# Four modulation units in one accumulator, 32 partitions each, against one unit at a time

## What is computed

```
cond = silu(c)                                             # 1 x 1024
mod = (cond @ w_ada[l] + b_ada[l]).reshape(b, 9, d)        # w_ada[l]: 1024 x 9216
kv_mod = (cond @ w_kv_ada + b_kv_ada).reshape(b, 2, d)     # once, for the shared K and V
h = modulate(x, mod[:, 0], mod[:, 1])                      # x * (1 + scale) + shift
x = post_norm_residual(x, swiglu(h, w_in, w_out), mod[:, 2], 0.5, ...)   # gate
```

## Time and profile before

| | us |
|---|---|
| median of 3 runs (1035.7 to 1037.51) | 1035.95 |
| span of the profiled execution | 1034.2 |
| PE busy | 1008.3 (97%) |
| DVE busy | 781.2 (76%) |
| ACT busy | 524.7 (51%) |
| POOL busy | 86.0 (8%) |
| DMA moved | 265.62 MB, 257 GB/s on average |

### The profile page before, as it was taken

How to read it: one execution, slowest core, us unless ns; L and a number is a source line. 1 busy time by engine, 2 the same in 40 slices (tenths; PEclk the granted TensorE clock), 3 DMA queues, 4 the chain that set the end, 5 groups by cost and what they waited for, 6 DMA issues and landing times.

```text
span 1034.2 us, 12480 instructions
## 1 busy us (share of the span) xinstructions
PE 1008.3 (97%) x4768; PEld 832.3 (80%) x4768; DVE 781.2 (76%) x915; ACT 524.7 (51%) x843; POOL 86.0 (8%) x160
## 2 busy tenths in 40 slices
PE   4999999999999999999999999999999999999997
PEld 3878888888888888888878888888888878888885
DVE  6888677879876897768887587777888977545485
ACT  1645453566465753545465644443568764434432
POOL 0011111000000011111000011111010010000000
PEclk9999999999999999999999999999999999999999
DMA  9999899846775499998928499989846748556541
GB/s 352 376 380 379 300 301 312 304 162 225 261 246 163 145 383 342 295 310 304 337 82 304 142 359 300 306 301 308 304 157 217 241 140 298 185 182 202 176 151 41
DMA packets 147491, 265.62 MB, mean 257 GB/s; under 512 B 8424, under 2 KB 98920, under 8 KB 147432
## 3 DMA queue, kind: packets, MB, share of 16 engines
q1 hardware_dynamic: 124448, 182.87, 52.2%
q0 software_dynamic: 20928, 75.53, 20.9%
q10 hardware_dynamic: 2056, 6.42, 1.9%
HBM read 263.75 MB, written 1.05 MB: 256 GB/s over the span
## 4 chain that ended last, share of the span: by engine, by line
PE 82%; DVE 9%; ACT 4%; issue 2%; DMA 2%; SPq 0%; DVEq 0%; ACTq 0%
PE psum L1419 17%; PE psum L1421 17%; PE psum L1420 17%; PE psum L1515 8%; PE psum L1517 8%; PE psum L1516 8%; DVE w_lo L951 2%; DMA raw<-in_w_ffn_in 2%; PE psum L1554 2%; ACT w_hi L584 1%; ACT psum L698 1%; DVE qT L1143 1%; PE psum L1454 1%; DVE qT L1144 1%; DVE tmp L972 1%
## 5 line engine op out<-in xcount | busy, mean ns | idle before, releaser
L951 DVE TENSOR_TENSOR w_lo<-raw,w_hi 128x2048 fp32r<-128x2048 f32 x164 | 371.5, 2286 | 61.2 <-ACT w_hi L584 61.1
L1419 PE MATMUL psum<-w_hi,hT_hi 128*128 128x512 f32 x896 | 355.6, 397 | 0.3
L1421 PE MATMUL psum<-w_hi,hT_lo 128*128 128x512 f32 x896 | 350.0, 391 | 0.0
L1420 PE MATMUL psum<-w_lo,hT_hi 128*128 128x512 f32 x896 | 349.0, 390 | 0.0
L584 ACT ACTIVATE w_hi<-raw 128x2048 fp32r<-128x2048 f32 x164 | 309.4, 1915 | 11.9 <-DMA raw<-in_w_ffn_in 9.6
L590 ACT ACTIVATE tmp<-psum 128x256 f32<-128x256 f32 x88 | 33.6, 383 | 338.4 <-PE psum L1421 338.4
L1421 PEld LDWEIGHTS psum<-w_hi,hT_lo 128*128 128x128 f32 x896 | 168.2, 188 | 35.9
L1419 PEld LDWEIGHTS psum<-w_hi,hT_hi 128*128 128x128 f32 x896 | 168.3, 188 | 35.4 <-issue 2.3
L1420 PEld LDWEIGHTS psum<-w_lo,hT_hi 128*128 128x128 f32 x896 | 168.5, 188 | 33.0
L1515 PE MATMUL psum<-w_hi,a_hi 128*128 128x512 f32 x368 | 147.8, 402 | 0.0
L1517 PE MATMUL psum<-w_hi,a_lo 128*128 128x512 f32 x368 | 143.8, 391 | 0.0
(11 more groups left out here) (166 smaller groups left out, 772.5 us busy)
## 6 DMA issues: line engine op xcount, KB each, us to landing
raw<-in_w_ffn_in SPq DMA_DIRECT2D x176, 512.0 KB, 5.6
raw<-in_w_ffn_out SPq DMA_DIRECT2D x88, 512.0 KB, 6.2
ada<-in_w_ada POOLq DMA_DIRECT2D x72, 512.0 KB, 6.0
qT<-in_w_ada POOLq DMA_DIRECT2D x56, 512.0 KB, 4.8
raw<-in_w_qkv_a SPq DMA_DIRECT2D x24, 512.0 KB, 4.8
raw<-in_w_o SPq DMA_DIRECT2D x16, 512.0 KB, 4.7
raw<-in_w_kv_b SPq DMA_DIRECT2D x16, 512.0 KB, 5.1
raw<-in_w_ada SPq DMA_DIRECT2D x4, 1024.0 KB, 16.3
```

What stands on the lines that cost most here:

```text
L951: nc.vector.tensor_tensor(lo_of(n), slot_of(n), hi_of(n).bitcast(F32), ALU.subtract)\
L1419: nc.tensor.matmul(dst, s_hi, m_hi, start=start, stop=False)
L1420: nc.tensor.matmul(dst, s_hi, m_lo, start=False, stop=False)
L1421: return nc.tensor.matmul(dst, s_lo, m_hi, start=False, stop=stop)
```

## The change

Four units (a quad: units 2 to 5, 8 to 11, 13 to 16) are summed at once in the one `acc`: unit i of the quad has partitions 32i to 32i + 31, with row 32p + r of its matrix on its partition p for load r of 32. The number of sums of 128x1024 on DVE stays 32 to a quad, and so do the bytes. Each row of a quad is now four DMAs of 32x1024 issued by POOL. `cond_quad` holds `cond` in that layout, four times; ACT loads and silus it at the start. PE turns `acc` once a quad, at step 8 (`STEPS - 3`), and DVE sums the turned tiles for all four units in one `tensor_reduce` (`keep_quad`); ACT's `keep_unit` is gone. At steps 2, 4 and 6 `turn_inner` writes to `misc` again and the additional waits fall away. The gates are as before. `zeros` has moved into `b_row`.

```diff
+QUAD_R = 32
...
-            loads[p] += 1
+            loads[p] += 1 if u in GATE_OF else 4
...
+        def quad_view(w):
+            return w.rearrange("(p r) n -> p r n", r=QUAD_R)
...
-                    pool.dma_start(ada_rows[place], ada_view(w)[:, row, j * D:(j + 1) * D])\
-                        .then_inc(ada_in[place], 16)
+                    if u in GATE_OF:
+                        pool.dma_start(ada_rows[place], ada_view(w)[:, row, j * D:(j + 1) * D])\
+                            .then_inc(ada_in[place], 16)
+                        continue
+                    step = 8 * (u - quad_first(u)) + row
+                    for i in range(4):
+                        of_layer, of_j = ORDER[quad_first(u) + i]
+                        of_w = w_kv_ada if of_layer == KV else w_ada[of_layer]
+                        pool.dma_start(ada_rows[place][32 * i:32 * i + 32, :],
+                                       quad_view(of_w)[:, step, of_j * D:(of_j + 1) * D])\
+                            .then_inc(ada_in[place], 16)
...
-            return FIRST_UNIT[f] is not None and s % 2 == 0 and 1 < s < STEPS - 1
+            return FIRST_UNIT[f] is not None and s == STEPS - 3
...
-                    if unit_turned(f, s):
-                        keep_unit(first_unit + s // 2 - 1)
...
+            for i in range(4):
+                act.dma_start(cond_quad[32 * i:32 * i + 32, :], c.rearrange("a (p r) -> p (a r)", r=QUAD_R))\
+                   .then_inc(c_quad_in, 16)
...
+            act.wait_ge(c_quad_in, 64)
+            nc.scalar.activation(cond_quad[:, :], cond_quad[:, :], ACT.Silu).then_inc(cond_quad_ready, 1)
...
+                    if u not in GATE_OF:
+                        step = 8 * (u - quad_first(u)) + 2 * q + r
+                        factor = cond_quad[:, step:step + 1]
...
+            def keep_quad(first):
+
+                dve.wait_ge(unit_out, sums_out(first + 3))
+                nc.vector.tensor_reduce(modT[:, first:first + 4, :].rearrange("p i k -> p k i"),
+                                        misc2.rearrange("p (k i q) -> p k i q", k=KT, i=4), AX.X, ALU.add)\
+                  .then_inc(mod_ready, 1)
...
                     inner_lo(f, s, 0)
+                    if unit_turned(f, s):
+                        keep_quad(first_unit)
                     quarter(s, 1)
...
-                        turn_unit(first_unit + s // 2 - 1)
+                        turn_unit(first_unit + 3)
```

More of the change, by code:

```diff
@@ L97, with quad_first, quads_kept, sums_out @@
 GATE_OF = [unit(0, 2), unit(0, 5), unit(0, 8), unit(1, 2), unit(1, 5), unit(1, 8)]
-def kept(u):
-    return sum(v not in GATE_OF for v in range(2, u + 1))
+QUAD_R = 32
+def quad_first(u):
+    return [v for v in (unit(0, 3), unit(KV, 0), unit(1, 3)) if v <= u][-1]
+def quads_kept(u):
+    return 1 + (unit(0, 3), unit(KV, 0), unit(1, 3)).index(quad_first(u))
+def sums_out(u):
+    return sum(v in GATE_OF or v == quad_first(v) + 3 for v in range(2, u + 1))
 FIRST_UNIT = [unit(0, 3), unit(KV, 0), unit(1, 3), None]
@@ L239, in build @@
         cond = sb("cond", [P, 8])
+        cond_quad = sb("cond_quad", [P, QUAD_R])
         total = sb("total", [P, 2 * TT])
@@ L247, in build @@
         neg_ones_r = sb("neg_ones_r", [P, P], F32R)
-        zeros = sb("zeros", [P, 256], BF16)
         masks = sb("masks", [P, 3, P], BF16)
@@ L258, in build @@
         acc0 = tmp[:, 512:1536]
+        zeros = b_row[:, 0:128].bitcast(BF16)
         ident = cst[:, C_ID:C_ID + P]
@@ L304, in build @@
         c_in = sem("c_in")
+        c_quad_in = sem("c_quad_in")
+        cond_quad_ready = sem("cond_quad_ready")
         rows_in = sem("rows_in")
@@ L596, in ffn @@
             def ffn(f):
-                first_unit, n = FIRST_UNIT[f], N_FFN[f]
+                n = N_FFN[f]
                 if f == 0:
@@ L642, in ffn @@
                 nc.scalar.preload_act_table(ACT.Sqrt)
[L644 to L652, removed]
             def gate_hi(i, last_use):
@@ L666, in keep_gate @@
             def keep_gate(i):
-                act.wait_ge(unit_out, GATE_OF[i] - 1)
+                act.wait_ge(unit_out, sums_out(GATE_OF[i]))
                 nc.scalar.activation(gate[:, :], misc2, ACT.Copy, scale=-GATE_W[i], bias=GATE_W[i])\
@@ L975, in accumulate @@
             def accumulate(u, q, rows=(0, 1)):
-                if q == 0 and 0 in rows:
+                first = u in GATE_OF or u == quad_first(u)
+                if first and q == 0 and 0 in rows:
                     if u == 2:
                         dve.wait_ge(start_sums, 2)
+                        dve.wait_ge(cond_quad_ready, 1)
                     else:
-                        dve.wait_ge(unit_out, u - 2)
+                        dve.wait_ge(unit_out, sums_out(u - 1))
                 for r in rows:
@@ L987, in accumulate @@
                     factor = cond[:, 2 * q + r:2 * q + r + 1]
-                    if q == 0 and r == 0:
+                    if u not in GATE_OF:
+                        step = 8 * (u - quad_first(u)) + 2 * q + r
+                        factor = cond_quad[:, step:step + 1]
+                    if first and q == 0 and r == 0:
                         if u not in GATE_OF:
@@ L1013, in gate_lo @@
                 nc.vector.tensor_tensor(sums_lo, acc[:, :], sums_hi.bitcast(F32), ALU.subtract).then_inc(sums_lo_ready, 1)
+            def keep_quad(first):
[3 more added lines that the diff above has]
+                  .then_inc(mod_ready, 1)
             def coefficients(i):
                 shift, scale, norm_i = H_OF[i]
-                dve.wait_ge(mod_ready, kept(scale))
+                dve.wait_ge(mod_ready, quads_kept(scale))
                 a, b = coef[:, i, 0, :], coef[:, i, 1, :]
@@ L1225, in _ @@
             nc.vector.memset(one[:, :], 1.0)
-            nc.vector.memset(zeros[:, :], 0.0).then_inc(set_up, 1)
+            nc.vector.memset(zeros, 0.0).then_inc(set_up, 1)
             dve.wait_ge(cond_ready, 1)
@@ L1595, in ffn @@
                     wide(pairs[s], 0)
-                    if first_unit is not None and s % 2 == 1 and 1 < s < STEPS - 1:
-                        pe.wait_ge(mod_ready, kept(first_unit + (s - 1) // 2 - 1))
+                    if unit_turned(f, s - 1):
+                        pe.wait_ge(mod_ready, quads_kept(first_unit))
                     turn_inner(f, s - 1, 1)
```

## The result

| | before | after |
|---|---|---|
| median, us | 1035.93 (4 runs, 1035.7 to 1037.51) | 1078.36 (4 runs, 1075.18 to 1082.98) |
| ratio | | 1.0413 (1.0398 to 1.0427) |
| span of the profiled execution | 1034.2 | 1075.0 |

What follows compares the result with a forecast made beforehand. PE, busy 97% of the span, was taken as the bound. Span 1034.2 - 7.8 (turnings) + 0.2 (second FFN's start) = 1026.6, with the runs' median 1.75 above the span: 1028.4 us; range 1026.3 to 1041.

Steps and rivals of the forecast that it cites:

- f: Time that ada bytes occupy the DMA engines after the change, against before; taken as 1, called the weakest term.
- The bounds, 1 and 2: Limits for f: 1 from same descriptors and engines, 2 from landing times of 4 KB and 512 KB loads.
- 13.3 + 5.4 (f - 1): DMA time of one FFN step in us, 5.4 of the 13.3 being ada; DMA bounds when it exceeds 16.85.
- The reserve of weights: Second and third FFN: five chunks of weights, some 22 us, would hide 15 us lost at f = 2.
- Rival (1): Quarter-size transfers hold the DMA longer, f = 2: start +5.4, six first-FFN steps +11.1, giving 1044.9 us; chance 0.16.
- The threshold, f = 1.66: FFN steps: DMA becomes the bound from here; between 1 and 1.66 only the first FFN's start pays, 1028.4 to 1032.
- The removal of nine turnings: PE in the FFNs: 9 of 12 turnings go, 0.87 us each, 7.8 us, all on the path.
- The reduce on DVE: Step 8 of each quad's FFN: one 128x1024 sum, taken as 1.2 us, hidden by DVE's idle time, costing nothing.
- POOL's issues: Quad steps: 384 issues for 96, 0.55 us each with the gap; POOL not the bound until one takes 1.05.
- The start of the second FFN: Two buffers come free at 355.5; late landing delays DVE's second sum, cost 0 to 1.6 us, taken as 0.2.
- The start of the program: Four more small ACT loads move the silu of cond some 1.5 us; the first split stays at 7.20; costs nothing.
- Rival (3): POOL or landing late: strong form 56 us, chance 0.02; mild DVE wait at second FFN's start, 1031 to 1033.

Runs made afterwards that it cites:

- e10_half_rows: e1_split32 with only half of the rows (row % 4 >= 2) split into four transfers, the others in one of 128 partitions: 1040.41 us, ratio 1.0037.
- e2_spread4: Changed kernel with unit i of a quad on every fourth partition (i, i + 4, ...) instead of 32 neighbouring; cond_quad and reduce follow: 1028.79 us, ratio 0.9926.
- e1_split32: Kernel before with each row of the FFNs' twelve units loaded in four transfers of 32 neighbouring partitions, all turnings kept: 1070.35 us, ratio 1.033.
- e7_spread_only: Kernel before with each row of the twelve units loaded in four transfers onto every fourth partition, all turnings kept: 1036.76 us, ratio 1.0005.
- e9_filler2: Changed kernel with the 72 removed transposes put back as idle work on PE at steps 2, 4 and 6: 1073.66 us, ratio 1.0361.

## Why the prediction was wrong, step by step

**The step that failed is f**, the time that ada bytes hold the DMA engines: taken as 1 "since the row length ... is unchanged", measured as 1.9 (223 for 416 GB/s). The length of the row was the wrong thing to look at. The bounds, 1 and 2, held for the loads by themselves, but the value was chosen by the row that looked nearest, and that row had nothing to say of partitions. The page of the Trainium skill that did ("SBUF — State Buffer", "Door 1: The DMA port swizzle"), with f = 1.74, was weighed and given less chance than the forecast; it was nearly right in the size of f.

f alone does not make the time. With 1.9 the prediction's own sum has 4.9 at the start and 7.9 in six steps, 1028.4 + 12.7 = 1041.1, where 1078.4 was measured. Two more of its terms were off:

```profile
654.00:723.00 69.00, 68.04 (x308) 55.81 (x307) 47.00 (x40) 21.75 (x24) 29.12 (x61) 1.00 1.06 265
```

- **The price beside other traffic.** At the 275 GB/s of 103 to 172 us the 5.2 MB of a step take 18.9 us, and at the 265 of this stretch in the third FFN 19.6. By the prediction's 13.3 + 5.4 (f - 1) that would be f = 2.0 to 2.2, an estimate from these rates: more than its upper bound.
- **The reserve of weights**, below.

**Rival (1) is what happened, at too low a price**: 1044.9 given, with f = 2, 1078.4 measured.
- The threshold, f = 1.66, agrees with the runs: at an average of 1.45 the loss was 4 us (`e10_half_rows`; the start's share was put at 2.4), at 1.9 it was 34. Where between the two it lies was not tested.
- The first FFN: 16.5 us of loss given. Measured 17.2 and, since the turnings there should have brought 2.6, 19.8. By PE's timeline 7.6 of it had been lost by the end of step 1 (its second `turn_inner` at 78.82, before at 71.21), for 5.4 given, and the other 12.2 for 11.1. About right, though with f = 1.9 only 12.7 would have been given.
- The second and third FFN: given as hidden by a reserve of 22 us, measured 13.9 and 9.5, with the turnings' share of 2.6 each some 16.5 and 12.1. This is the larger error. PE's timeline shows where it fell in the third FFN, in step 0, at the end of step 5 and in step 9; of before:

```profile
590.71 0.38 PE L1554 MATMUL psum<-cst,tmp 128*128 128x128 f32 x2
...
682.37 0.38 PE L1554 MATMUL psum<-cst,tmp 128*128 128x128 f32 x2
...
740.37 0.38 PE L1554 MATMUL psum<-cst,tmp 128*128 128x128 f32 x2
```

and after:

```profile
621.86 0.38 PE L1588 MATMUL psum<-cst,tmp 128*128 128x128 f32 x2
...
711.71 0.38 PE L1588 MATMUL psum<-cst,tmp 128*128 128x128 f32 x2
...
781.04 0.38 PE L1588 MATMUL psum<-cst,tmp 128*128 128x128 f32 x2
```

Up to the end of step 5 PE lost nothing: 89.85 us for 91.66, less by the two turnings that are gone. Then it took 69.33 us for 58.00. So the reserve seems to have carried PE through six steps and then to have run out. Eight steps of 19.6 for 16.85 us make 22 us of lateness, an estimate, where the prediction had 15; 12.1 were lost, so that about 10 were taken in, where it had 22. In the second FFN PE had lost 1.2 us by the end of step 3 (at 425.67, before at 408.17), and the rest came in steps 4 to 8. There the kernel before moved 353 GB/s at 379 to 413 us to refill and the changed one 267, so the reserve was smaller from the start; that is read from the traces and was not tested by a run.

- The clock was left out of the rival. `e2_spread4` has the same 4696 instructions on PE as the changed kernel, and PE is busy for 1000.7 us there and 1015.3 here, and idle for 25.1 and 59.7. So of the 49.2 us between their spans 34.6 are waits and 14.6 are slower work, which goes with a mean granted clock of 0.995 and 0.980.

**The removal of nine turnings**, 7.8 us: right where PE sets the pace. `e2_spread4` is 7.2 us faster than the kernel before beside it (1028.79 to 1036.01), the prediction had 7.6. Its trace has one piece in the chain for each FFN, of the size of the earlier trace rows:

```profile
177.81 0.87 PE psum L1488 x8
```

Where the DMA sets the pace it was worth nothing: the changed kernel is 8 us slower than `e1_split32`, which has all twelve. Why it is even slower is only in part explained, as said.

**The reduce on DVE**, 1.2 us, hidden: right. In `e2_spread4` DVE is idle for 0.99 us behind it before 190.27, and PE works on. It took 1.22 in step 8 of the first FFN after:

```profile
200.50 1.22 DVE L1043 TENSOR_REDUCE modT<-psum 128x32 f32<-128x1024 f32 x1
```

**POOL's issues**, taken as 0.55: 0.50 in the first eight here, and they never bound.

```profile
40.95 4.02 POOL L529 DMA_DIRECT2D ada<-in_w_ada  x8 [40.51 <-ACT w_hi L611]
```

**The start of the second FFN**, 0.2 us: `e2_spread4`, where nothing else disturbs it, shows DVE waiting 0.20 us for the second load, and PE goes on.

```profile
360.23 1.28 DVE L1024 SCALAR_TENSOR_TENSOR acc<-qT,cond_quad,acc 128x1024 f32<-128x1024 f32 x1 [0.20 <-DMA qT<-in_w_ada]
```

**The start of the program**: the silu of `cond` moved by 2.1 us, where 1.5 was given, and the first split from 7.20 to 7.41. Nothing, as said.

```profile
6.22 0.21 ACT L765 ACTIVATE cond<-cond 128x8 f32<-128x8 f32 x1 [3.87 <-issue]
7.41 1.91 ACT L611 ACTIVATE w_hi<-raw 128x2048 fp32r<-128x2048 f32 x1 [0.99 <-DMA raw<-in_w_ffn_in]
```

**Rival (3)**, POOL, is out by the same rows and by `e7_spread_only`.

**Two slips in its sums**, which did not move the forecast: three reduces without cover would be 3 x 1.2 = 3.6 us, not 1.2; and by the sums of rival (1) the result is over 0.2% slower from f = 1.82 on, not 1.9.

## What to carry to other kernels

When a layout puts several small things side by side on the partitions, ask which partitions one transfer reaches, and not only how long its rows are: `i:128:4` and `32i:32i+32` have the same bytes, number and issues and differ here by 34 to 50 us. If a transfer type does not occur in the trace, its rate cannot be taken from the nearest row; a few lines of loads in a kernel of their own price it. And a cost on a shared resource can have a threshold, worked out from its load against the pace of the bound: here half of the bad transfers cost 4 us and all of them 34. A reserve only puts the loss off: ask how many steps it lasts.

## What had not been expected of the hardware

- Transfers into one half of the partitions slow the other queue too: at 48 to 52 us the total fell from 392 to 252 GB/s, and the weights' landing from a median of 5.6 to 12.2 us, though their own transfers span all 128 partitions. The packets of SP's queue took 54.4% of 1075.0 us, 585 us, for 52.2% of 1034.2, 540 us, at the same 182.87 MB.
- The 32 partitions need not be many or near: every fourth one comes near the full rate (386 GB/s in the kernel, for 392 before), every second one of a half does not (21.20 us by itself, as 32 neighbours).
- The order 0, 2, 1, 3 gives 7% by itself and takes 14 of 50 us away in the kernel.
- More work on PE made a kernel faster (`e9_filler2`, by 4.7 us).
